# The last block's first down product among the last up products, read from PSUM by VectorE

## The chip, the cores and the metric

One core of a Trainium2 chip runs the whole program. The metric is device time in microseconds (us), from the first to the last instruction and what lies around them, as the median of several executions. Smaller is better.

## The reference

The reference is a two-layer trunk over 512 tokens of 1024 channels in fp32: a mixer, cross-attention into 256 memory tokens, and a squared-ReLU MLP in each layer, every one behind an RMSNorm, with a final RMSNorm. What matters here is the MLP, which both layers have:

```
def squared_relu_mlp(h, w1, w2):          # h (512 x 1024), w1 (1024 x 4096), w2 (4096 x 1024)
    return jnp.square(jax.nn.relu(h @ w1)) @ w2
...
h = rmsnorm(x, norm_ffn_g[i])
x = x + squared_relu_mlp(h, ffn_w1[i], ffn_w2[i])
...
return rmsnorm(x, final_norm_g)
```

## The kernel before

**Blocks and products.** The 4096 hidden channels are worked in FB = 4 blocks of 1024, numbered 0 to 3. A block has an up product (`"U"`, tokens x 1024 by 1024 x 1024) and a down product (`"D"`). Each is a 2 x 2 block matrix product done with seven quarter-size products, P1 to P7, instead of eight (Winograd's form): the operands of some are sums of quarters, the results of several are accumulated in one pair of PSUM banks and read at stages. Each product has two halves and each half is one *step*: 12 matmuls of 128x512 for a down step, 24 matmuls of 128x256 for an up step. fp32 accuracy comes from three matmuls on operands split in a high and a low part: ScalarE writes the high part of a weight (`w_hi`, L748), VectorE the low part (`w_lo`, L1253), and the same for activations (`slot_hi` L762, `slot_lo` L1263).

**Weights.** The split weights lie in a ring of RING = 4. `ahead(kind, b, p, half)` makes the split for the step three behind the named one (AHEAD = 3), so ScalarE writes a split when TensorE has finished the step four before it. The raw quarter of a weight comes from HBM into a buffer: `sum` (`w_sum[:, 0:2]`), `22` and `21`. In the `sum` buffer P1 uses the quarter 11 as loaded; then GpSimd issues an accumulating DMA (`add_quarters`, L1942) that adds the next quarter in place, for P5, then for P6, then P4. In `22`, P3 uses what was loaded and P7 what it is after one addition. An addition may start when the split of the step before it has been made (`wlo_ready`). SP loads the next block's quarters when the last reader of a buffer has made its split (`refill`, L633).

**Order.** The order of steps is written out by hand and every engine follows it: `ORDER` for the blocks, `LAST_UPS` for the stretch where up products of block 3 alternate with down products of block 2, `LAST_DOWN` for the rest of block 3. There P1 of block 3 comes second, behind half of P2: 466.44 us is the first matmul of D P4 of block 2 in layer 0, and P2.0, P1.0, P1.1, P5.0, P5.1, P3.0, P3.1, P6.0, P6.1, P2.1, P7.0, P7.1, P4.0, P4.1 follow it.

**Results.** Down results are added to the residual rows in `y_rows` in SBUF. For most, VectorE reads PSUM, scales and adds (`read`, L1621). Three of a layer are *staged* (`STAGED`): ScalarE scales PSUM into `staged` in SBUF (`stage`, L979), and GpSimd issues a DMA that adds it to `y_rows` (`add_staged`, L1953). They are P4 of block 2 and P1 and P5 of block 3. P3 of block 3 goes on accumulating in the PSUM banks of P5, so TensorE waits before P3.0, tile by tile, until P5 has been staged; P6 accumulates behind P1, P7 behind P6, P4 behind P7, each after the reading before it.

**Queues.** ScalarE, VectorE, GpSimd and SP each work strictly in their written order. In ScalarE's, the splits for P3.1 and P6.0 stand around the staging of P1 and before that of P5. In GpSimd's, the additions for P5, P3 and P6 of block 3 have a staged one behind P1's, P5's and P3's.

**Start of the MLP.** Up P5 of block 0 is kept in SBUF in two halves by ScalarE (`keep`, L925, counting `kept_half` and `kept_ready`). TensorE waits before step U P3.0 for the first half, and for `sum_done(0, "P2")`, which is VectorE's sum at L1538.

**Behind the MLP of layer 0.** The rows are transposed back into tiles (`tiles_from_rows`) in banks that `mlp_order` and `walk` name, and the gate product `sv` starts in banks that must have been copied out.

Of the kernel before, what the change touches and what calls it, by code (L numbers as in the profile page):

```python
# [22 lines left out]
ALU = mybir.AluOpType  # L23
# [33 lines left out]
LAST_DOWN = (("P2", 0), ("P1", 0), ("P1", 1), ("P5", 0), ("P5", 1), ("P3", 0), ("P3", 1), ("P6", 0), ("P6", 1),  # L57
             ("P2", 1), ("P7", 0), ("P7", 1), ("P4", 0), ("P4", 1))
LAST_UPS = (("D", "P1"), ("U", "P1"), ("D", "P2"), ("U", "P2"), ("D", "P5"), ("U", "P5"), ("D", "P3"), ("U", "P3"),
            ("U", "P6"), ("D", "P6"), ("U", "P7"), ("D", "P7"), ("U", "P4"), ("D", "P4"))  # L60
READS = {b: ("P1", "P2", "P5", "P3", "P6", "P7", "P4") for b in range(FB - 2)}
READS[FB - 2] = ("P1", "P2", "P5", "P3", "P6", "P7")
READS[FB - 1] = ("P3", "P6", "P2", "P7", "P4")
STAGED = ((FB - 2, "P4"), (FB - 1, "P1"), (FB - 1, "P5"))


def mlp_steps():

    steps = [("U", 0, p, h) for p in ORDER for h in range(2)]
    for b in range(FB - 2):  # L70
        for p in ORDER:
            steps += [("D", b, p, h) for h in range(2)] + [("U", b + 1, p, h) for h in range(2)]
    steps += [(kind, FB - 2 + (kind == "U"), p, h) for kind, p in LAST_UPS for h in range(2)]
    return tuple(steps + [("D", FB - 1, p, h) for p, h in LAST_DOWN])

# [24 lines left out]
LAST_SLOTS = {"P2": 0, "P5": 1, "P1": 2, "P3": 2, "P6": 1, "P7": 2, "P4": 1}  # L100
# [51 lines left out]
class Numbers:  # L152
# [64 lines left out]
    def walk(self):  # L217
# [84 lines left out]
    def mlp_order(self, l):  # L302
# [37 lines left out]
def trunk_kernel(nc, x_t, x_rows, mem_t, weights, up_d, down_d, gains_d, ws_t, bs_d, lng_d, lnb_d, ident_d, band_d, last_gain_d, out):  # L340
# [90 lines left out]
    staged = [at(a_off + 16 * KB + 4 * KB * i, f"staged_{i}", [P, 2, 512]) for i in range(3)]  # L431
# [90 lines left out]
    quarter_added = [sem(f"quarter_added{i}") for i in range(4)]  # L522
    up_loaded = [sem(f"up_loaded{i}") for i in range(6)]
# [14 lines left out]
    rows_added = sem("rows_added")  # L538
# [41 lines left out]
    def buffer(kind, i):  # L580

        if kind == "D":
# [39 lines left out]
    with nc.Block() as block:  # L622

        @block.sync
        def _(sp):
# [3 lines left out]
            def quarter(l, kind, b, name, half):  # L629
# [3 lines left out]
                sp.dma_start(buffer(kind, i), source[FB * l + b, 2 * QUARTERS.index(name) + half]).then_inc(loaded[i], 16)  # L633
# [46 lines left out]
            def mlp_loads(l):  # L680
# [44 lines left out]
        def _(act):  # L725
# [10 lines left out]
            def hi_quarter(c):  # L736
# [6 lines left out]
                if added == 0:  # L743
                    act.wait_ge(loaded[i], 16 * (FB * l + b + 1))
                else:
                    sums = 3 if part == "sum" else 1
                    act.wait_ge(adds[i], 16 * (sums * (FB * l + b) + added))
                act.activation(w_hi[:, c % RING, :], buffer(kind, i), ACT.Copy).then_inc(whi_ready, 1)  # L748
# [165 lines left out]
            def mlp(l):  # L914
# [180 lines left out]
                stage(1)  # L1095
                ahead("D", b, "P5", 1)
                stage(2)
# [132 lines left out]
        def _(dve):  # L1230
# [15 lines left out]
            def lo_any(c):  # L1246
# [6 lines left out]
                dve.tensor_tensor(w_lo[:, c % RING, :], buffer(kind, SUM_BUFFER[STAGE[p][0]] + half),  # L1253
# [257 lines left out]
            def mlp(l, stat, norm):  # L1511
# [86 lines left out]
                def read(b, p, tile_waits=False):  # L1598
# [3 lines left out]
                    if (b, p) == (FB - 1, "P2"):  # L1602
                        dve.wait_ge(rows_added, added_count(l, 1))
                    elif (b, p) == (FB - 1, "P7"):
                        dve.wait_ge(rows_added, added_count(l, 2))
                    elif (b, p) == (FB - 1, "P4"):
                        dve.wait_ge(rows_added, added_count(l, 0))
# [139 lines left out]
                operand(c, "P1", a11)  # L1747
# [41 lines left out]
            def last_rows():  # L1789
# [775 lines left out]
```

## Time and profile before

| what | value |
|---|---|
| median of 3 runs | 1162.18 us (1161.82 to 1162.69) |
| the profiled execution, its time | 1160.81 us |
| the profiled execution, span from first to last instruction | 1159.0 us |
| TensorE busy | 1134.8 us, 98% |
| VectorE, ScalarE, GpSimd busy | 810.3, 653.6, 212.0 us |
| mean granted TensorE clock | 0.998 of full |

Busy shares are averages. TensorE's has matmuls that overlap their neighbours, so the start of a matmul less the start of the one before it says more than its duration: in an undisturbed down step these starts lie about 0.227 us apart. A row of the timeline has in brackets the idle time before an instruction and the engine and line that ended it.

### The profile page before, as it was taken

Reading aid. Unit: us, or ns where it says so; the run is one execution under the profiler, and the core shown is the slowest. Engines: PE = TensorE matmul, PEld = TensorE weight load, DVE = VectorE, ACT = ScalarE, POOL = GpSimd, SP = SyncE. Lnnn points to the kernel's source line nnn. Section 1 sums busy time; section 2 is a strip of 40 time slices with the busy share of each in tenths; the row PEclk is TensorE's granted clock in tenths of the full one; section 3 lists DMA queues with packets and bytes.
Section 4 is the critical chain, followed back from the end, with each engine's and each line's share of the span. In section 5 each row is a group of like instructions: output and inputs, shape, how many; then the busy total and the mean of one; then the engine's idle time right before and its main releaser. Section 6 shows DMA issues by size and latency. Waiting matters only on the chain.

```text
span 1159.0 us, 16201 instructions
## 1 busy us (share of the span) xinstructions
PE 1134.8 (98%) x6556; PEld 1000.2 (86%) x6556; DVE 810.3 (70%) x923; ACT 653.6 (56%) x811; POOL 212.0 (18%) x196
## 2 busy tenths in 40 slices
PE   9999999999999999899999999999999999999996
PEld 7988889999999999688888888888999999999974
DVE  7887646686786776677487645664668678677677
ACT  6764445765655565655444443544576565556565
POOL 0040012112111120212164012001311211112030
PEclk9999999999999999999999999999999999999999
DMA  9532143899789785856232622313489978978585
GB/s 353 206 97 91 50 146 73 198 245 197 190 175 213 171 153 115 214 118 198 89 98 81 217 96 73 109 37 146 77 221 231 206 182 179 211 167 153 125 157 146
DMA packets 50378, 179.75 MB, mean 155 GB/s; under 512 B 5632, under 2 KB 6016, under 8 KB 49664
## 3 DMA queue, kind: packets, MB, share of 16 engines
q0 software_dynamic: 20064, 70.26, 33.6%
q1 hardware_dynamic: 28656, 104.35, 27.1%
q10 hardware_dynamic: 1584, 4.10, 1.1%
q8 instruction: 52, 0.85, 0.3%
q14 instruction: 22, 0.18, 0.1%
HBM read 173.45 MB, written 2.10 MB: 151 GB/s over the span
## 4 chain that ended last, share of the span: by engine, by line
PE 83%; DVE 7%; ACT 4%; DMA 3%; issue 2%; POOL 1%; SPq 0%; ACTq 0%; DVEq 0%; POOLq 0%
PE psum L2004 12%; PE psum L2006 11%; PE psum L2005 11%; PE psum L2264 8%; PE psum L2266 8%; PE psum L2265 8%; PE psum L2284 7%; PE psum L2285 7%; PE psum L2286 7%; DMA w_sum<-in_down 3%; ACT w_hi L748 1%; DMA w_raw<-in_weights 1%; PE psum L2201 1%; DVE w_lo L1253 1%; PE psum L2323 1%
## 5 line engine op out<-in xcount | busy, mean ns | idle before, releaser
L1253 DVE TENSOR_TENSOR w_lo<-w_sum,w_hi 128x1024 fp32r<-128x1024 f32 x112 | 136.0, 1223 | 82.2 <-ACT w_hi L748 82.1
L2284 PE MATMUL psum<-w_lo,slot_hi 128*128 128x512 f32 x448 | 176.0, 393 | 9.8 <-ACT staged L979 5.0
L2285 PE MATMUL psum<-w_hi,slot_hi 128*128 128x512 f32 x448 | 175.5, 392 | 0.0
L2286 PE MATMUL psum<-w_hi,slot_lo 128*128 128x512 f32 x448 | 174.9, 390 | 0.0
L748 ACT ACTIVATE w_hi<-w_sum 128x1024 fp32r<-128x1024 f32 x112 | 117.6, 1054 | 93.7 <-PE psum L2286 52.8
L2264 PE MATMUL psum<-xs_s_lo,w_hi 128*128 128x256 f32 x512 | 145.4, 284 | 2.7 <-ACT kept_p L925 2.7
L2266 PE MATMUL psum<-xs_s_hi,w_lo 128*128 128x256 f32 x512 | 144.9, 283 | 0.0
L2265 PE MATMUL psum<-xs_s_hi,w_hi 128*128 128x256 f32 x512 | 144.9, 283 | 0.0
L1253 DVE TENSOR_TENSOR w_lo<-w_raw,w_hi 128x1024 fp32r<-128x1024 f32 x80 | 97.6, 1222 | 41.9 <-ACT w_hi L748 41.7
L748 ACT ACTIVATE w_hi<-w_raw 128x1024 fp32r<-128x1024 f32 x80 | 83.8, 1055 | 69.0 <-PE psum L2266 56.8
L1942 POOL DMA_DIRECT2D w_sum<-in_down x64 | 58.6, 942 | 343.9 <-DVE w_lo L1253 343.8
L2284 PEld LDWEIGHTS psum<-w_lo,slot_hi 128*128 128x128 f32 x448 | 84.7, 189 | 28.5 <-issue 10.7
L2266 PE MATMUL psum<-xs_a_hi,w_lo 128*128 128x256 f32 x384 | 108.7, 283 | 0.0
L2265 PE MATMUL psum<-xs_a_hi,w_hi 128*128 128x256 f32 x384 | 108.7, 283 | 0.0
L2264 PE MATMUL psum<-xs_a_lo,w_hi 128*128 128x256 f32 x384 | 108.6, 283 | 0.0
L2264 PEld LDWEIGHTS psum<-xs_s_lo,w_hi 128*128 128x128 f32 x512 | 98.2, 192 | 3.9 <-issue 3.0
L2286 PEld LDWEIGHTS psum<-w_hi,slot_lo 128*128 128x128 f32 x448 | 84.5, 189 | 18.0
L2265 PEld LDWEIGHTS psum<-xs_s_hi,w_hi 128*128 128x128 f32 x512 | 98.2, 192 | 0.9
L2285 PEld LDWEIGHTS psum<-w_hi,slot_hi 128*128 128x128 f32 x448 | 84.6, 189 | 15.9
L2266 PEld LDWEIGHTS psum<-xs_s_hi,w_lo 128*128 128x128 f32 x512 | 98.2, 192 | 0.0
L1239 DVE TENSOR_TENSOR w_lo<-w_raw,w_hi 128x1024 fp32r<-128x1024 f32 x58 | 76.1, 1319 | 19.5 <-ACT w_hi L734 19.5
L2004 PE MATMUL psum<-a_lo,w_hi 128*128 128x512 f32 x192 | 75.9, 395 | 0.0
(236 smaller groups left out, 2662.4 us busy)
## 6 DMA issues: line engine op xcount, KB each, us to landing
w_raw<-in_weights SPq DMA_DIRECT2D x89, 512.0 KB, 3.7
w_sum<-in_down POOLq DMA_DIRECT2D x64, 512.0 KB, 7.7
w_sum<-in_down SPq DMA_DIRECT2D x48, 512.0 KB, 4.5
w_raw<-in_up POOLq DMA_DIRECT2D x48, 512.0 KB, 6.6
w_raw<-in_up SPq DMA_DIRECT2D x32, 512.0 KB, 3.9
up<-in_up SPq DMA_DIRECT2D x16, 512.0 KB, 4.5
up<-in_up POOLq DMA_DIRECT2D x16, 512.0 KB, 6.9
y_rows<-staged POOLq DMA_DIRECT2D x6, 512.0 KB, 8.0
```

Source lines behind the costliest of these rows:

```text
L748: act.activation(w_hi[:, c % RING, :], buffer(kind, i), ACT.Copy).then_inc(whi_ready, 1)
L1239: dve.tensor_tensor(w_lo[:, slot, :], w_raw[:, raw, :], w_hi[:, slot, :].bitcast(F32), ALU.subtract).then_inc(wlo_ready, 1)
L1253: dve.tensor_tensor(w_lo[:, c % RING, :], buffer(kind, SUM_BUFFER[STAGE[p][0]] + half), w_hi[:, c % RING, :].bitcast(F32), ALU.subtract).t ...
L2004: pe.matmul(out_ap, s_hi, m_lo, start=start, stop=False)
L2005: pe.matmul(out_ap, s_hi, m_hi, start=False, stop=False)
L2006: return pe.matmul(out_ap, s_lo, m_hi, start=False, stop=stop)
L2264: pe.matmul(to, h[:, k, tile], x_lo[:, k, :], start=fresh and m == k == 0, stop=False, skip_group_check=True)
L2265: pe.matmul(to, h[:, k, tile], x_hi[:, k, :], start=False, stop=False, skip_group_check=True)
L2266: last = pe.matmul(to, lw[:, k, tile], x_hi[:, k, :], start=False, stop=(k == 3), skip_group_check=True)
L2284: pe.matmul(to, s_hi[:, k, tok], w_lo[:, c % RING, cols], start=first, stop=False, skip_group_check=True)
L2285: pe.matmul(to, s_hi[:, k, tok], w_hi[:, c % RING, cols], start=False, stop=False, skip_group_check=True)
L2286: last = pe.matmul(to, s_lo[:, k, tok], w_hi[:, c % RING, cols], start=False, stop=(kp == 1 and j == 1), skip_group_check=True)
```

## The change

P1 of block 3 is moved from the last down steps to the last up products, between D P7 of block 2 and U P4 of block 3. Its weights (and those of P5, P6, P4 of block 3 after it) no longer lie in `w_sum[:, 0:2]` but in `up_22`, the up products' buffer, free after U P7 of block 3, with semaphores `last_added` of their own. P4 of block 2 and P1 of block 3 are no longer staged; VectorE reads them. Only P5 of block 3 is staged. PSUM pairs, slots and transpose banks are renamed to fit. In the MLP's start, ScalarE keeps the first half of up P5 two instructions earlier.

```diff
-LAST_DOWN = (("P2", 0), ("P1", 0), ("P1", 1), ("P5", 0), ("P5", 1), ("P3", 0), ("P3", 1), ("P6", 0), ("P6", 1),
+LAST_DOWN = (("P2", 0), ("P5", 0), ("P5", 1), ("P3", 0), ("P3", 1), ("P6", 0), ("P6", 1),
              ("P2", 1), ("P7", 0), ("P7", 1), ("P4", 0), ("P4", 1))
+LAST_UPS = tuple((kind, FB - 2 + (kind == "U"), p) for p in ("P1", "P2", "P5", "P3") for kind in "DU") + (
+    ("U", FB - 1, "P6"), ("D", FB - 2, "P6"), ("U", FB - 1, "P7"), ("D", FB - 2, "P7"), ("D", FB - 1, "P1"),
+    ("U", FB - 1, "P4"), ("D", FB - 2, "P4"))
-STAGED = ((FB - 2, "P4"), (FB - 1, "P1"), (FB - 1, "P5"))
+STAGED = ((FB - 1, "P5"),)
-LAST_SLOTS = {"P2": 0, "P5": 1, "P1": 2, "P3": 2, "P6": 1, "P7": 2, "P4": 1}
+LAST_SLOTS = {"P1": 0, "P2": 1, "P5": 0, "P3": 2, "P6": 0, "P7": 2, "P4": 0}
-    return {PAIR_X: PAIR_A, PAIR_Y: PAIR_E if p == "P2" else PAIR_Y}[ROWS_PAIR[p]]
+    return {PAIR_X: PAIR_E, PAIR_Y: PAIR_A if p == "P2" else PAIR_Y}[ROWS_PAIR[p]]
-            self.add(("xt", m), "bank", at=(4, 5, 2, 3)[m])
+            self.add(("xt", m), "bank", at=4 + m)
-            self.row_chunk("sv", i, ST, at=(0, 1, 6, 7, 5, 2, 3, 4))
+            self.row_chunk("sv", i, ST, at=(0, 1, 2, 3, 5, 6, 7, 4))
-                self.add(("xt", m), "bank", at=(6, 7, 0, 1)[m - 4])
+                self.add(("xt", m), "bank", at=m - 4)
...
+        if (kind, b) == ("D", FB - 1) and i < 2:
+            return up_22[:, i, :]
...
@@ SP: the loads of the last block @@
+                refill(l, "D", FB - 2, "P2")
+                for half in range(2):
+                    sp.wait_ge(wlo_ready, step(l, "U", FB - 1, "P7", half) + 1)
+                    quarter(l, "D", FB - 1, "11", half)
+                refill(l, "D", FB - 2, "P7")
@@ ScalarE: start of the MLP @@
                 ahead("U", 0, "P5", 0)
+                keep(0, "P5", kept_p5, PAIR_X, half=0)
                 hi(xs["P4"][0][:], xg[:, 4:8, TOK[1]])
                 ahead("U", 0, "P5", 1)
-                keep(0, "P5", kept_p5, PAIR_X, half=0)
@@ ScalarE: the last block @@
                 ahead("U", c, "P7", 0)
-                operand(c, "P2", a12, h=1)
+                operand(c, "P1", a11, h=0)
                 ahead("U", c, "P7", 1)
-                squared(c, 2, a22, "P7")
                 ahead("D", b, "P7", 0)
                 ahead("D", b, "P7", 1)
+                squared(c, 2, a22, "P7")
+                ahead("D", c, "P1", 0)
+                operand(c, "P2", a12, h=1)
+                ahead("D", c, "P1", 1)
...
                 operand(c, "P5", s1, summed=1)
-                operand(c, "P1", a11, h=0)
                 b = FB - 1
                 ahead("D", b, "P2", 0)
-                stage(0)
-                ahead("D", b, "P1", 0)
-                ahead("D", b, "P1", 1)
                 operand(b, "P3", a12, summed=3)
                 ahead("D", b, "P5", 0)
...
-                stage(1)
                 ahead("D", b, "P5", 1)
-                stage(2)
+                stage(0)
                 operand(b, "P6", last_s2, summed=2)
@@ VectorE: the last block @@
                 read(b, "P6")
+                operand(c, "P1", a11)
+                ahead("U", c, "P7", 1)
+                ahead("D", b, "P7", 0)
+                c22(c)
+                ahead("D", b, "P7", 1)
+                ahead("D", c, "P1", 0)
+                read(b, "P7")
                 operand(c, "P2", a12)
-                ahead("U", c, "P7", 1)
-                c22(c)
-                ahead("D", b, "P7", 0)
-                ahead("D", b, "P7", 1)
+                ahead("D", c, "P1", 1)
                 ahead("U", c, "P4", 0)
-                read(b, "P7")
+                read(c, "P1")
...
                 operand(c, "P5", s1)
-                operand(c, "P1", a11)
                 b = FB - 1
                 ahead("D", b, "P2", 0)
                 last_sum_s4(b)
-                ahead("D", b, "P1", 0)
-                ahead("D", b, "P1", 1)
+                read(b - 1, "P4")
                 operand(b, "P3", a12)
+                ahead("D", b, "P5", 0)
                 sum_s3(b)
-                ahead("D", b, "P5", 0)
@@ GpSimd @@
-                        elif p != "P6":
-                            add_staged(l, ("P1", "P5", "P3").index(p))
+                        elif p == "P3":
+                            add_staged(l, 0)
@@ TensorE @@
                 down_product(b, "P7")
+                kept_done(c, "P3")
+                down_product(c, "P1", fresh=True)
                 sum_done(c, "P7")
                 up_product(c, "P4")
                 read_done(b, "P7")
                 down_product(b, "P4")
                 b = FB - 1
-                kept_done(b, "P3")
+                kept_done(b, "P4")
                 down(b, "P2", 0, fresh=True).then_inc(psum_ready, 1)
-                kept_done(b, "P4")
-                down_product(b, "P1", fresh=True)
...
-                pe.wait_ge(staged_ready, 6 * l + 4)
+                read_done(b, "P1")
                 down_product(b, "P6")
```

## Rows read from the trace of the kernel before

**Rows 1.** The page: busy us, share of the span and instructions by engine.
```profile
PE 1134.8 (98%) x6556; PEld 1000.2 (86%) x6556; DVE 810.3 (70%) x923; ACT 653.6 (56%) x811; POOL 212.0 (18%) x196
```
**Rows 2.** Waits of TensorE: who released it, us in total, times, longest.
```profile
PE psum L2284 <- ACT staged L979: 5.0, 2, 4.0
PE psum L2284 <- DVE y_rows L1621: 2.8, 2, 1.7
PE psum L2264 <- ACT kept_p L925: 2.7, 2, 1.3
PE psum L2284 <- DVE slot_lo L1263: 2.1, 2, 1.1
```
**Rows 3.** Timeline, TensorE, layer 0's last block: start, duration, instruction [idle <- releaser].
```profile
466.44 0.40 PE L2284 MATMUL psum<-w_lo,slot_hi 128*128 128x512 f32 x1
...
471.90 0.39 PE L2284 MATMUL psum<-w_lo,slot_hi 128*128 128x512 f32 x1
...
475.75 0.47 PE L2284 MATMUL psum<-w_lo,slot_hi 128*128 128x512 f32 x1 [0.96 <-DVE slot_lo L1263]
...
490.83 0.58 PE L2284 MATMUL psum<-w_lo,slot_hi 128*128 128x512 f32 x1 [3.95 <-ACT staged L979]
...
511.56 0.39 PE L2284 MATMUL psum<-w_lo,slot_hi 128*128 128x512 f32 x1
```
**Rows 4.** Windows: stretch, us, busy by engine, granted TensorE clock, DMA share, GB/s.
```profile
491.00:495.00 4.00, 4.00 (x11) 3.11 (x11) 2.73 (x3) 2.16 (x3) 2.24 (x3) 0.57 1.10 183
```
**Rows 5.** Timeline, ScalarE, the same stretch.
```profile
489.06 1.06 ACT L748 ACTIVATE w_hi<-w_sum 128x1024 fp32r<-128x1024 f32 x1 [3.81 <-DMA w_sum<-in_down]
490.02 1.25 ACT L979 ACTIVATE staged<-psum,negative_r 128x512 f32<-128x512 f32 x2
```
**Rows 6.** The chain of waits through that stretch: start, us, what.
```profile
469.88 7.74 DMA w_sum<-in_down
...
481.24 7.74 DMA w_sum<-in_down
```
**Rows 7.** Timeline, TensorE, layer 1's last block.
```profile
1101.72 0.40 PE L2284 MATMUL psum<-w_lo,slot_hi 128*128 128x512 f32 x1
...
1145.71 0.47 PE L2284 MATMUL psum<-w_lo,slot_hi 128*128 128x512 f32 x1 [1.69 <-DVE y_rows L1621]
```
**Rows 8.** Timeline, VectorE, layer 0: split for U P7.0, low part of P5's operand.
```profile
442.41 1.23 DVE L1253 TENSOR_TENSOR w_lo<-up,w_hi 128x1024 fp32r<-128x1024 f32 x1 [1.66 <-ACT w_hi L748]
...
473.25 1.22 DVE L1263 TENSOR_TENSOR slot_lo<-s,slot_hi 128x1024 fp32r<-128x1024 f32 x1
```
**Rows 9.** Timeline, ScalarE, layer 0: split for U P4.0 of block 3.
```profile
452.54 1.06 ACT L748 ACTIVATE w_hi<-w_raw 128x1024 fp32r<-128x1024 f32 x1 [0.60 <-PE psum L2266]
```
**Rows 10.** Tile staged: its DMAs, from issue to landing.
```profile
DMA to landing us min/median/max: 5.4/8.0/12.0
```
**Rows 11.** Timeline, ScalarE, layer 1: splits for P6.0 and P4.1 of block 3.
```profile
1121.55 1.06 ACT L748 ACTIVATE w_hi<-w_sum 128x1024 fp32r<-128x1024 f32 x1 [1.43 <-DMA w_sum<-in_down]
...
1141.44 1.06 ACT L748 ACTIVATE w_hi<-w_sum 128x1024 fp32r<-128x1024 f32 x1 [1.40 <-DMA w_sum<-in_down]
```
**Rows 12.** Timeline, VectorE, layer 1, before P4: gain of the first rows, reading of P7.
```profile
1143.68 1.22 DVE L1508 TENSOR_TENSOR out_rows<-y_rows,last_gain 128x1024 f32<-128x1024 f32 x1
1144.82 1.40 DVE L1621 SCALAR_TENSOR_TENSOR y_rows<-psum,negative_r,y_rows 128x512 f32<-128x512 f32 x2
```
**Rows 13.** Timeline, TensorE, first matmul of the gate product.
```profile
519.13 0.47 PE L2004 MATMUL psum<-w_lo,a_hi 128*128 128x512 f32 x1 [0.20 <-issue]
```
**Rows 14.** Timeline, TensorE, layer 0: step U P3.0 of block 0.
```profile
208.80 0.36 PE L2264 MATMUL psum<-xs_s_lo,w_hi 128*128 128x256 f32 x1 [1.33 <-ACT kept_p L925]
```
**Rows 15.** Timeline, ScalarE, before that step.
```profile
206.06 1.05 ACT L762 ACTIVATE xs_a_hi<-xg 128x1024 fp32r<-128x1024 f32 x1
...
207.96 0.58 ACT L925 ACTIVATE kept_p<-psum 128x512 f32<-128x512 f32 x1
```
**Rows 16.** Timeline, VectorE, before that step: the sum of up P1 and P2.
```profile
206.58 1.22 DVE L1538 TENSOR_TENSOR a<-psum,kept 128x1024 f32<-128x1024 f32 x1
```

More of the change, by code:

```diff
@@ L72, in mlp_steps @@
             steps += [("D", b, p, h) for h in range(2)] + [("U", b + 1, p, h) for h in range(2)]
-    steps += [(kind, FB - 2 + (kind == "U"), p, h) for kind, p in LAST_UPS for h in range(2)]
+    steps += [(kind, b, p, h) for kind, b, p in LAST_UPS for h in range(2)]
     return tuple(steps + [("D", FB - 1, p, h) for p, h in LAST_DOWN])
@@ L430, in trunk_kernel @@
     last_s2 = at(z_off, "last_s2", [P, 4, NMEM])
-    staged = [at(a_off + 16 * KB + 4 * KB * i, f"staged_{i}", [P, 2, 512]) for i in range(3)]
+    staged = [at(a_off + 16 * KB + 4 * KB * i, f"staged_{i}", [P, 2, 512]) for i in range(len(STAGED))]
     edge_lo = at(region(GROUPS * PAD * 4), "edge_lo", [P, GROUPS, PAD], F32R)
@@ L522, in trunk_kernel @@
     quarter_added = [sem(f"quarter_added{i}") for i in range(4)]
+    last_added = [sem(f"last_added{i}") for i in range(2)]
     up_loaded = [sem(f"up_loaded{i}") for i in range(6)]
@@ L537, in trunk_kernel @@
     staged_ready = sem("staged_ready")
-    rows_added = sem("rows_added")
+    rows_added = [sem(f"rows_added{i}") for i in range(len(STAGED))]
     tile_ready = sem("tile_ready")
@@ L578, in first_raw, with buffer @@
         return N.raw[C[f"o{l}"] + 7] + 1
-    def buffer(kind, i):
+    def buffer(kind, b, i):
+        if (kind, b) == ("D", FB - 1) and i < 2:
+            return up_22[:, i, :]
         if kind == "D":
@@ L632, in quarter @@
                 source, loaded = (up_d, up_loaded) if kind == "U" else (down_d, quarter_loaded)
-                sp.dma_start(buffer(kind, i), source[FB * l + b, 2 * QUARTERS.index(name) + half]).then_inc(loaded[i], 16)
+                sp.dma_start(buffer(kind, b, i), source[FB * l + b, 2 * QUARTERS.index(name) + half]).then_inc(loaded[i], 16)
             def refill(l, kind, b, p):
@@ L744, in hi_quarter @@
                     act.wait_ge(loaded[i], 16 * (FB * l + b + 1))
-                else:
-                    sums = 3 if part == "sum" else 1
-                    act.wait_ge(adds[i], 16 * (sums * (FB * l + b) + added))
-                act.activation(w_hi[:, c % RING, :], buffer(kind, i), ACT.Copy).then_inc(whi_ready, 1)
+                elif part != "sum":
+                    act.wait_ge(adds[i], 16 * (FB * l + b + added))
+                elif kind == "U":
+                    act.wait_ge(up_added[i], 16 * (3 * (FB * l + b) + added))
+                elif b < FB - 1:
+                    act.wait_ge(quarter_added[i], 16 * (3 * ((FB - 1) * l + b) + added))
+                else:
+                    act.wait_ge(last_added[i], 16 * (3 * l + added))
+                act.activation(w_hi[:, c % RING, :], buffer(kind, b, i), ACT.Copy).then_inc(whi_ready, 1)
             def hi_any(c):
@@ L1252, in lo_any @@
                 dve.wait_ge(whi_ready, c + 1)
-                dve.tensor_tensor(w_lo[:, c % RING, :], buffer(kind, SUM_BUFFER[STAGE[p][0]] + half),
+                dve.tensor_tensor(w_lo[:, c % RING, :], buffer(kind, b, SUM_BUFFER[STAGE[p][0]] + half),
                                   w_hi[:, c % RING, :].bitcast(F32), ALU.subtract).then_inc(wlo_ready, 1)
@@ L1938, in add_quarters @@
                 source, added = (up_d, up_added) if kind == "U" else (down_d, quarter_added)
+                if kind == "D" and b == FB - 1 and part == "sum":
+                    added = last_added
                 for half in range(2):
@@ L1941, in add_quarters @@
                     pool.wait_ge(wlo_ready, step(l, kind, b, p, half) + 1)
-                    pool.dma_start(buffer(kind, i), source[FB * l + b, 2 * QUARTERS.index(name) + half],
+                    pool.dma_start(buffer(kind, b, i), source[FB * l + b, 2 * QUARTERS.index(name) + half],
                                    accum_op=ALU.add).then_inc(added[i], 16)
@@ L1948, in add_staged @@
                 part = ROWS_PART[p]
-                pool.wait_ge(rows_read, read_count(l, FB - 2, {"P4": "P7", "P1": "P2", "P5": "P7"}[p]))
-                if p == "P4":
-                    pool.wait_ge(rows_read, read_count(l, FB - 3, "P4"))
-                pool.wait_ge(staged_ready, 2 * (3 * l + i) + 2)
-                pool.dma_start(y_part(*part), staged[i][:], accum_op=ALU.add).then_inc(rows_added, 16)
+                pool.wait_ge(rows_read, read_count(l, FB - 2, "P7"))
+                pool.wait_ge(staged_ready, 2 * l + 2)
+                pool.dma_start(y_part(*part), staged[i][:], accum_op=ALU.add).then_inc(rows_added[i], 16)
             def mlp(l):
@@ L2429, in mlp @@
                     read_done(b, "P7")
-                    pe.wait_ge(staged_ready, 2)
                     tiles_from_rows(4)
```

32 lines of the change are left out of this document (10 added, 22 removed).

## The prediction

> **What bounds the kernel now.** I read the page first: TensorE is busy 98% of the span and no other engine over 70% [rows 1]. So the time is TensorE's own work, which the change leaves alone (the same steps in another order), and the places where it waits; its idle time comes to 1159.0 less 1134.8, 24 us, its end included. I then asked for TensorE's waits [rows 2]: the reader sees 12.6 us in four groups of two waits; for `y_rows` both are in layer 1, for the others there is one per layer. Three groups lie in the last block, the fourth (`kept_p`) at the start of the MLP, and the change touches all of them.
>
> Third, TensorE's timeline in layer 0 [rows 3]. From the start of D P4 of block 2 (466.44) the next two steps take 5.46 us (to 471.90), so a down step is worth 2.72 us undisturbed. Up to the last product, P4 of block 3 (511.56), lie 14 such steps, 38.1 us, but 45.1 us pass: 7.0 us are lost. They are 1.1 us before P1.0 (475.75), 4.1 us before P3.0 (490.83), and some 1.7 us behind it, because there the granted clock read 0.57 of full for 4 us [rows 4], that is mostly at the lower of its two levels, 1.2 GHz. What the engine did before the clock fell is the idle 3.95 us. In layer 1 the same 14 steps take 44.0 us [rows 7], so 5.9 us are lost there in four shorter waits of 1.0 to 1.7 us [rows 2], with no fall visible.
>
> Fourth, what ended the long wait. ScalarE staged P5 at 490.02, directly behind its split of P6.0's weights at 489.06, for which it had stood 3.81 us behind a DMA [rows 5]. The chain shows that DMA: the addition for P6.0, issued at 481.24 and 7.74 us in flight, and before it the addition for P5.0, issued at 469.88, also 7.74 us [rows 6]. So P1 split, add, P5 split, add, P6 split is one serial chain, and its start is tied to P1, whose buffer is busy until D P4 of block 2. TensorE doesn't need P6.0's weights yet: it waits for a staging that is queued behind them.
>
> **The change part by part.**
>
> *P1 two steps earlier.* TensorE's D P4 of block 2 starts 5.44 us later (466.44 becomes 471.9), P2.0 at 477.3, P5.0 at 480.05, P3.0 at 485.5. P1.0's split now takes the ring slot that U P4.0 had, at 452.5 [rows 9]; its addition is issued some 3 us later, near 456, and is wanted for P5.0's split near 472. With 7.74 us in flight [rows 6] it is there 8 us early. P5.0's split takes P1.0's old place in the pattern, 5.44 us later, so its addition is issued at 469.88 + 5.44 = 475.3. It lands at 483.0 with 7.74 us, at 480.7 with the 5.4 us that is the shortest landing of a like DMA [rows 10]. P6.0's split can't start before 484.2 for another reason (below). The 4.1 us wait loses its cause.
>
> *P1's load.* SP may issue it when U P7.0 is split, at 442.41 + 1.23 = 443.6 [rows 8]; the split wants it at 452.5 [rows 9]. It has 8.9 us. The rows show no load of this kind late there; if it took the 12.0 us of the longest landing in rows 10, the stall would be 3.1 us.
>
> *P5's operand.* Its low part ended at 473.25 + 1.22 = 474.47 [rows 8], behind U P4 and the square. It moves with U P4 by 5.44 us to 479.9, and TensorE wants it at 480.05. So the 1.1 us wait, which was for P1's low part queued one operation behind, goes to about nothing; bounds 0 and 0.3 us.
>
> *What is late next.* P3.0 waits for the staging of P5. ScalarE's order before it: P3's operand, split P3.1, split P6.0, staging. P3's operand waits for VectorE, which after 479.9 makes the split of P3.0 and the sum for P3, 1.14 us apart in a busy VectorE: done 482.2. Then three ScalarE operations at 0.96 us each (489.06 to 490.02 in [rows 5]): staging of the first tile starts at 485.15, ends 485.8, and TensorE follows 0.15 us later, at 485.95 where it wanted 485.5. I take 0.45 us as the new wait, per layer; bounds 0 and 1.5 us (a late addition).
>
> *VectorE's new readings.* It reads P1 and P4 of block 2, 1.40 us each [rows 12], where ScalarE staged both. The one of P1 falls at about 468.5, between two splits that wait for ScalarE anyway. The one of P4 stands between the sum for P3 and P3's low part: that ends at 484.6, before 485.5. If its cover were gone it would cost 1.4 us. Nothing else of TensorE's waits for either: P6 waits for P1's reading 20 us later.
>
> *Two staged DMAs fewer.* From the landing that released P6.0's split in layer 1 (1121.5) to the one that released P4.1's (1141.4) seven GpSimd DMAs landed, 2.84 us each [rows 11]; the queue was full, so every split there stood behind it. After, the additions and the one staging are issued at (layer 0's scale) 475.3, 478.5, 482.0, 486.7, 487.4, 488.9 and 491.2. With 5.6 us for one alone and 2.84 us between two in a full queue, the last two land at 497.7 and 500.6. Their splits are wanted at 496.8 and 499.6, but TensorE starts P4 only at 505.0. In layer 0 this costs nothing. In layer 1 VectorE does 1.22 us of gain before it reads P7 [rows 12]; the split of P4.1 ends near 503.3, the gain at 504.4, and the first tile of P7 is read at 505.2, against a wanted 504.9. I take 0.5 us; bounds 0 and 3.
>
> At this place the Trainium skill speaks against the change ("DMA: Bandwidth & Descriptors", Issuing engines are not separate DMA queues): transfers from the SP, ScalarE and GpSimd queues run on the same 16 engines and interleave. By it ScalarE's load of the last gain in layer 1, issued just ahead of the additions, pushes them back by up to one service time, and the 0.5 us would be some 3; the row of the window above has the engines' share at 1.1 with GpSimd's DMAs in flight, which agrees that there is no room beside a full queue.
>
> *Sum in the last blocks.* Layer 0: 7.0 less 0.45 is 6.6 us. The clock's 1.7 us is in it: with no wait over 1.7 us left, the layer 1 block shows no fall. Layer 1: 5.9 less 0.45 less 0.5, and less 0.3 because VectorE's tail behind the reading of P7 sits 0.3 us later against TensorE's than now: 4.65 us.
>
> *Keeping half of up P5 earlier.* ScalarE kept it at 207.96, behind two operations from 206.06 on [rows 15]; now it does so at 206.06 and is done at 206.65. TensorE started at 208.80 [rows 14] and wanted 207.3. But it also waits for VectorE's sum, 206.58 to 207.80 [rows 16], so it starts at 207.95: 0.85 us gained, 1.7 us in two layers. Bounds 0 and 3.0 (1.5 each). ScalarE's operations behind it keep their times, as it never idled there.
>
> *Gate product.* It idled 0.20 us before its first matmul [rows 13], behind the copy of the tile in its bank, which is now the first copied instead of the third: 0.35 us with the start-up of the matmul; bounds 0 and 0.4.
>
> Sum: 6.6 + 4.65 + 1.7 + 0.35 = 13.3 us. Against the profiled execution's own time (1160.81, span 1159.0) that is 1147.5; this execution lies 1.4 us below the median, so on the median 1162.18 the forecast is 1148.9 us.
>
> **The rivals.**
>
> *A: the wait comes back at the same place.* P6.0's split still stands before the staging in ScalarE's order. If P5.0's addition lands 12.0 us after issue [rows 10] instead of 5.4 to 7.7, that is 487.3, the staging ends at 489.1, TensorE waits 3.7 us and the clock falls as before: 5.4 us back in layer 0 less the 0.45 counted, as much in layer 1. For it: many landings were that long. Against: those were behind a full queue, and at 475.3 this one is alone. Gain left 13.3 - 10 = 3.3 in both layers, 8.3 in one: 1153.9 to 1158.9 us.
>
> *B: the last additions are late.* They are issued from 489 to 491 behind P3's and the staged one. With landings of 12 us the split of P4.1 ends at 505.5 and the reading of P7 slips 1.5 us in layer 0 and 2.7 in layer 1: 4 us less the 0.5 counted, so 1152.4 us. For it: rows 11, and the skill's rule above. Against: two staged DMAs fewer are ahead of them, and P5's additions are out of the queue by then.
>
> *C: slower than before.* P1's load sits in front of everything: split, addition, and ScalarE's whole queue wait for it. It has 8.9 us, and each us more is a us of TensorE in each layer. It cancels the gain when it lands 8.9 + 6.7 = 15.6 us after issue in both; at 18 us the kernel would take 1148.9 + 2 x 9.1 = 1167 us. The longest landing of the rows is 12.0 us.
>
> *D: no change.* TensorE at 98% is its own bound and what is taken from one wait appears in the next engine's order, because ScalarE and VectorE have no room for operations in another order. VectorE's 70% [rows 1] speaks against it. 1162 us.
>
> **How the numbers follow.** Forecast (gain 11 to 16 us, all bounds of the small terms) 0.63; A 0.12; B 0.15; C 0.05; D 0.05. If every bound falls well, the gain is 7.0 + 5.9 + 3.0 + 0.4 = 16.3 us, 1145.9; the range reaches on the other side through B and one layer of A: 1145.8 to 1155.0. What a measurement of this kernel can tell from no change is about 0.2%, 2.3 us. Faster: forecast, A, B and a little of D, 0.91. Same 0.04, slower 0.05.
>
> **What would show it.** In the changed kernel's profile TensorE's wait behind `staged` should be under 1 us in each layer, the window with a clock of 0.57 gone, the waits behind `kept_p` gone and one of some 0.6 us behind L1538 in their place, ScalarE's waits for `w_sum` DMAs in the last block (the 3.81 us one first) gone or shifted to the last two splits. From D P4 of block 2 to P4 of block 3 there should be 33 us in layer 0. I would be wrong if TensorE waits at D P1 of block 3 (its load), at U P4 behind VectorE, or if a wait over 3 us is left anywhere in the last block.

## The result, and the profile after

| | before | after |
|---|---|---|
| median of the runs side by side, us | 1162.43 (1161.82 to 1165.84, 4 runs) | 1147.90 (1147.83 to 1148.66, 4 runs) |
| profiled execution, us | 1160.81 | 1147.92 |
| its span, us | 1159.0 | 1146.0 |
| its mean granted clock | 0.998 | 0.999 |

The changed kernel takes 0.9871 of the time before (95% interval 0.9851 to 0.9890): 14.5 us less by the medians, 12.9 us less between the two profiled executions. The forecast was 1148.9 us, in a range from 1145.8 to 1155.0.

The page of the changed kernel, its engines and its GpSimd queue, answers to [rows 1]. TensorE has as many matmuls as before and is busy 2.3 us less; the queue carries 68.17 MB, against 70.26 in the kernel before.

```profile
PE 1132.5 (99%) x6556; PEld 998.9 (87%) x6556; DVE 815.6 (71%) x931; ACT 648.9 (57%) x803; POOL 207.0 (18%) x192
...
q0 software_dynamic: 18976, 68.17, 33.0%
```

TensorE's waits in it (released by, us in total, times, longest) answer to [rows 2]:

```profile
PE psum L2084 <- DVE warm L1369: 1.5, 1, 1.5
PE psum L2203 <- DVE probs L1482: 1.3, 2, 0.6
PE psum L2006 <- DVE w_lo L1248: 1.1, 2, 0.7
PE psum L2266 <- issue: 0.9, 2, 0.4
PE psum L2006 <- DVE mem_lo L1269: 0.4, 1, 0.4
```

All four groups of [rows 2] are gone, 12.6 us of named waits. The one at L2266 is what is left before U P3.0 of block 0. The last line, at the start of the program, stood nowhere in the list of before.

TensorE's timeline in the last block of layer 0, against [rows 3]: start, duration, instruction.

```profile
471.49 0.40 PE L2286 MATMUL psum<-w_lo,slot_hi 128*128 128x512 f32 x1
...
484.99 0.39 PE L2288 MATMUL psum<-w_hi,slot_lo 128*128 128x512 f32 x1
485.50 0.47 PE L2286 MATMUL psum<-w_lo,slot_hi 128*128 128x512 f32 x1
...
504.64 0.39 PE L2286 MATMUL psum<-w_lo,slot_hi 128*128 128x512 f32 x1
...
511.62 0.39 PE L2288 MATMUL psum<-w_hi,slot_lo 128*128 128x512 f32 x1
511.85 0.39 PE L2006 MATMUL psum<-w_lo,a_hi 128*128 128x512 f32 x1
```

The rows are D P4 of block 2 (471.49), D P3.0 of block 3 (485.50), D P4 of block 3 (504.64) and the gate product (511.85). From the first to the third 33.15 us pass, where 33 were forecast and twelve undisturbed steps of 2.72 us [rows 3] take 32.6. Matmuls follow each other every 0.23 us, so the start at 485.50 instead of 485.22 is 0.28 us lost: too short for the trace to print as a wait, but there. The gate product follows its predecessor without a gap, unlike in [rows 13].

The windows of it (us, busy by engine, clock, DMA share, GB/s). The first spans the place of the old 4 us wait, the second is that of [rows 4], which had the clock at 0.57:

```profile
484.00:488.00 4.00, 3.88 (x18) 2.91 (x17) 4.00 (x5) 3.94 (x5) 1.92 (x3) 1.00 0.70 110
491.00:495.00 4.00, 4.00 (x19) 3.30 (x19) 3.73 (x5) 3.04 (x3) 0.08 (x1) 1.00 1.10 194
```

The clock is granted in full, and 19 matmuls start where 11 did. ScalarE in layer 0 answers to [rows 5, 9]:

```profile
452.15 1.06 ACT L756 ACTIVATE w_hi<-up 128x1024 fp32r<-128x1024 f32 x1 [0.60 <-PE psum L2268]
...
481.83 1.06 ACT L770 ACTIVATE slot_hi<-a 128x1024 fp32r<-128x1024 f32 x1 [3.61 <-DVE a L1582]
482.79 1.04 ACT L756 ACTIVATE w_hi<-w_sum 128x1024 fp32r<-128x1024 f32 x1
483.74 1.04 ACT L756 ACTIVATE w_hi<-up 128x1024 fp32r<-128x1024 f32 x1
484.69 1.42 ACT L987 ACTIVATE staged<-psum,negative_r 128x512 f32<-128x512 f32 x2
```

The split of P1.0 stands where that of U P4.0 stood. The split of P6.0 (483.74) no longer waits for a DMA; ScalarE's long idle time is now 3.61 us behind VectorE's sum for P3, and the four operations behind it run without a pause. That is the new chain before P3.0: VectorE's sum, P3's operand, two splits, the staging.

In layer 1, TensorE before P3.0 and before P4, against [rows 7]:

```profile
1112.36 0.39 PE L2288 MATMUL psum<-w_hi,slot_lo 128*128 128x512 f32 x1
1112.90 0.47 PE L2286 MATMUL psum<-w_lo,slot_hi 128*128 128x512 f32 x1
...
1131.83 0.39 PE L2288 MATMUL psum<-w_hi,slot_lo 128*128 128x512 f32 x1
1132.24 0.47 PE L2286 MATMUL psum<-w_lo,slot_hi 128*128 128x512 f32 x1
```

Lost: 0.31 us and 0.18 us, against 5.9 us in the whole block before. One split there still waits for an addition, that of P4.1 on ScalarE (against [rows 11]):

```profile
1127.46 1.06 ACT L756 ACTIVATE w_hi<-up 128x1024 fp32r<-128x1024 f32 x1 [1.30 <-DMA up<-in_down]
```

and it sets VectorE's readings of P7 before P4 (against [rows 12]):

```profile
1129.08 1.22 DVE L1259 TENSOR_TENSOR w_lo<-up,w_hi 128x1024 fp32r<-128x1024 f32 x1
1130.21 1.22 DVE L1514 TENSOR_TENSOR out_rows<-y_rows,last_gain 128x1024 f32<-128x1024 f32 x1
1131.35 0.74 DVE L1623 SCALAR_TENSOR_TENSOR y_rows<-psum,negative_r,y_rows 128x512 f32<-128x512 f32 x1
```

Last, U P3.0 of block 0 in both layers, on TensorE (against [rows 14]):

```profile
208.43 0.36 PE L2266 MATMUL psum<-xs_s_lo,w_hi 128*128 128x256 f32 x1 [0.43 <-issue]
...
835.84 0.35 PE L2266 MATMUL psum<-xs_s_lo,w_hi 128*128 128x256 f32 x1 [0.43 <-issue]
```

### The profile page after: what moved, and what is told of

The parts are those of the page before. It is cut to its first block, busy times and chain, and to the rows that moved or that the text cites. A ratio compares the mean times of both kernels' runs of the same rounds, so it can differ in the third digit from the quotient of the medians.

```text
span 1146.0 us, 16195 instructions
## 1 busy us (share of the span) xinstructions
PE 1132.5 (99%) x6556; PEld 998.9 (87%) x6556; DVE 815.6 (71%) x931; ACT 648.9 (57%) x803; POOL 207.0 (18%) x192
## 3 DMA queue, kind: packets, MB, share of 16 engines
q0 software_dynamic: 18976, 68.17, 33.0%
## 4 chain that ended last, share of the span: by engine, by line
PE 90%; DVE 6%; ACT 2%; issue 1%; DMA 1%; POOL 0%; SPq 0%; DVEq 0%; POOLq 0%; ACTq 0%
PE psum L2006 12%; PE psum L2007 12%; PE psum L2008 12%; PE psum L2266 9%; PE psum L2268 9%; PE psum L2267 9%; PE psum L2286 8%; PE psum L2287 8%; PE psum L2288 8%; DMA w_raw<-in_weights 1%; PE psum L2203 1%; DVE w_lo L1259 1%; PE psum L2325 1%; DVE w_lo L1248 1%; POOL sq L1995 0%
## 5 line engine op out<-in xcount | busy, mean ns | idle before, releaser
L1259 DVE TENSOR_TENSOR w_lo<-w_sum,w_hi 128x1024 fp32r<-128x1024 f32 x96 | 116.9, 1223 | 65.2 <-ACT w_hi L756 65.1
L2266 PE MATMUL psum<-xs_s_lo,w_hi 128*128 128x256 f32 x512 | 145.4, 284 | 0.9 <-issue 0.9
L756 ACT ACTIVATE w_hi<-w_sum 128x1024 fp32r<-128x1024 f32 x96 | 101.2, 1055 | 69.6 <-PE psum L2288 56.4
L2266 PE MATMUL psum<-xs_a_lo,w_hi 128*128 128x256 f32 x384 | 108.6, 283 | 0.0
L2266 PEld LDWEIGHTS psum<-xs_s_lo,w_hi 128*128 128x128 f32 x512 | 98.1, 192 | 2.1 <-issue 1.2
L1946 POOL DMA_DIRECT2D w_sum<-in_down x52 | 44.8, 862 | 290.6 <-DVE w_lo L1259 290.4
```

Of the source, the lines that this page charges most:

```text
L756: act.activation(w_hi[:, c % RING, :], buffer(kind, b, i), ACT.Copy).then_inc(whi_ready, 1)
L1259: dve.tensor_tensor(w_lo[:, c % RING, :], buffer(kind, b, SUM_BUFFER[STAGE[p][0]] + half), w_hi[:, c % RING, :].bitcast(F32), ALU.subtract ...
L2266: pe.matmul(to, h[:, k, tile], x_lo[:, k, :], start=fresh and m == k == 0, stop=False, skip_group_check=True)
```

## The experiments

The theory under test: before, one serial chain on ScalarE and the GpSimd queue (P1 split, add, P5 split, add, P6 split, staging) started too late, and the change starts it two steps earlier; the missing staged DMAs matter less (unstaged_only and moved_staged show how far that holds). Seven kernels, each beside runs of the kernel before.

| kernel | median, us | of before | ratio (95%) |
|---|---|---|---|
| keep_only | 1160.61 | 1161.93 | 0.9989 (0.9980 to 0.9997) |
| before_swap | 1161.36 | 1161.93 | 0.9995 (0.9985 to 1.0005) |
| unstaged_only | 1153.40 | 1161.93 | 0.9921 (0.9908 to 0.9935) |
| moved_staged | 1148.50 | 1162.77 | 0.9879 (0.9865 to 0.9894) |
| late_load | 1147.69 | 1162.77 | 0.9874 (0.9859 to 0.9889) |
| after_swap | 1146.96 | 1161.93 | 0.9870 (0.9856 to 0.9883) |
| swap_gain_early | 1146.85 | 1162.77 | 0.9867 (0.9851 to 0.9884) |

### keep_only: the earlier keeping alone

```
+                keep(0, "P5", kept_p5, PAIR_X, half=0)
                 hi(xs["P4"][0][:], xg[:, 4:8, TOK[1]])
                 ahead("U", 0, "P5", 1)
-                keep(0, "P5", kept_p5, PAIR_X, half=0)
```

> The kernel before with one edit: ScalarE keeps the first half of up P5 two instructions earlier. My step says TensorE's wait at step U P3.0 of block 0 shrinks to what VectorE's sum leaves, 0.85 us less in each layer: 1.7 us less in all, near 1160.6 us if before is 1162.3. Rival: TensorE waits for something else there to the same moment, 0 us. Upper bound, both waits gone: 3.0 us.

Measured: 1.3 us less, with an interval of 0.3 to 2.3, in which the 1.7 expected lies. TensorE at U P3.0, and in its last blocks:

```profile
207.97 0.36 PE L2264 MATMUL psum<-xs_s_lo,w_hi 128*128 128x256 f32 x1 [0.43 <-issue]
...
490.25 0.60 PE L2284 MATMUL psum<-w_lo,slot_hi 128*128 128x512 f32 x1 [4.16 <-ACT staged L979]
...
1144.35 0.47 PE L2284 MATMUL psum<-w_lo,slot_hi 128*128 128x512 f32 x1 [1.98 <-DVE y_rows L1621]
```

U P3.0 starts 0.83 us earlier than in [rows 14], and its wait is 0.9 us shorter in both layers; the waits in the last blocks are all still there. The term holds by itself. In layer 1 the wait before P4 is 1.98 us instead of the 1.69 of [rows 7], and the clock falls behind it (window of this kernel). That takes the gain back in this one profiled execution, whose span is 1159.2 us:

```profile
1145.50:1149.50 4.00, 4.00 (x13) 3.11 (x12) 2.82 (x6) 2.52 (x8) 0.00 (x0) 0.57 0.00 2
```

### before_swap: is it the order on ScalarE alone?

The long wait was a staging queued behind a split that TensorE didn't need yet. So the cheapest cure would be to exchange the two.

```
                 stage(1)
-                ahead("D", b, "P5", 1)
                 stage(2)
+                ahead("D", b, "P5", 1)
```

> The kernel before with P5's staging ahead of the split of P6.0 in ScalarE's order, nothing else. Rival theory, the order of ScalarE's queue alone made the loss: the 4.1 us wait before P3.0 and the clock's 1.7 us go in layer 0, some 5.4 us less in layer 0 and 0.7 in layer 1, near 1156 us. My theory, a full queue of accumulating DMAs stands behind it: the wait before P3.0 goes, but P6's additions still land at about 505 and 507, VectorE's split of P4.1 ends near 509.8 and P7 is read only behind it, so TensorE starts P4 at about 510.7 instead of 511.56: under 1.5 us less in layer 0 and nothing in layer 1, near 1161.3 us.

Measured: no difference that can be told (ratio 0.9995, the interval holds 1). The wait before P3.0 did go, and came back later: from D P1.0 to D P4.0 of block 3 the profiled execution needs 35.37 us, where the kernel before needs 35.81. TensorE in layer 0:

```profile
494.03 0.47 PE L2284 MATMUL psum<-w_lo,slot_hi 128*128 128x512 f32 x1 [0.67 <-DVE slot_lo L1263]
504.83 0.50 PE L2284 MATMUL psum<-w_lo,slot_hi 128*128 128x512 f32 x1 [2.35 <-DVE y_rows L1621]
```

ScalarE behind it shows why, with the additions late one after the other:

```profile
498.65 1.06 ACT L748 ACTIVATE w_hi<-w_sum 128x1024 fp32r<-128x1024 f32 x1 [2.79 <-DMA w_sum<-in_down]
501.13 1.06 ACT L748 ACTIVATE w_hi<-w_sum 128x1024 fp32r<-128x1024 f32 x1 [1.42 <-DMA w_sum<-in_down]
...
506.37 1.06 ACT L748 ACTIVATE w_hi<-w_sum 128x1024 fp32r<-128x1024 f32 x1 [3.23 <-DMA w_sum<-in_down]
509.00 1.06 ACT L748 ACTIVATE w_hi<-w_sum 128x1024 fp32r<-128x1024 f32 x1 [1.58 <-DMA w_sum<-in_down]
```

In layer 1 this execution took 2.0 us longer than before between U P3.0 of block 0 and P4 of block 3, with 2.59 us of idle time before P4, but also with 1.82 us before P1.0, ahead of the exchanged operations, and a fall of the clock behind it; one trace doesn't say what of this is the edit's.

The rival (the order alone is the cause) is out. The chain through the GpSimd queue was late as a whole; the staging was only the place where TensorE felt it first.

### unstaged_only: VectorE reads two results, P1 stays where it was

```
-STAGED = ((FB - 2, "P4"), (FB - 1, "P1"), (FB - 1, "P5"))
+STAGED = ((FB - 1, "P5"),)
...
-                stage(0)
                 ahead("D", b, "P1", 0)
...
+                read(b, "P4")
                 b = FB - 1
                 ahead("D", b, "P2", 0)
...
                 ahead("D", b, "P5", 1)
+                read(b, "P1")
```

> The kernel before with P4 of block 2 and P1 of block 3 read by VectorE instead of staged (two accumulating DMAs fewer per layer); P1 stays where it was, as do its weights' buffer and the other orders. My theory: the addition for P6.0 is issued at about 480.9 and lands at 486.6 instead of 489.0, TensorE starts P3.0 at 488.5 (a wait of 1.8 us, no fall of the clock), and the last additions land 4 us earlier: 4.1 us less in layer 0, some 3.5 in layer 1, the 1.1 us wait before P1.0 stays in both, near 1154.8 us. Rival, the earlier start of P1's chain is the whole gain: the wait before P3.0 stays near 4 us and the kernel is within 2 us of before.

Measured: 8.5 us less, where 7.6 were expected (4.1 and 3.5); the two profiled spans differ by 7.5. TensorE in layer 0, then ScalarE:

```profile
475.80 0.47 PE L2275 MATMUL psum<-w_lo,slot_hi 128*128 128x512 f32 x1 [0.96 <-DVE slot_lo L1260]
488.39 0.47 PE L2275 MATMUL psum<-w_lo,slot_hi 128*128 128x512 f32 x1 [1.43 <-ACT staged L978]
```

```profile
486.62 1.06 ACT L747 ACTIVATE w_hi<-w_sum 128x1024 fp32r<-128x1024 f32 x1 [1.83 <-DMA w_sum<-in_down]
487.58 1.25 ACT L978 ACTIVATE staged<-psum,negative_r 128x512 f32<-128x512 f32 x2
```

The wait before P1.0 in layer 0 is that of [rows 3] to a hundredth (in layer 1 it is 1.39 us, before 1.10): it belongs to P1's place, not to the staging. The one before P3.0 fell from 3.95 to 1.43 us, as the addition for P6.0, issued at 480.94, was there 5.7 us later and not 7.74 [rows 6]; and behind 1.43 us the clock did not fall. So the chain is the same, and the emptier queue shortens it.

### moved_staged: P1 moved and with its own buffer, three results still staged

```
-STAGED = ((FB - 1, "P5"),)
+STAGED = ((FB - 1, "P1"), (FB - 2, "P4"), (FB - 1, "P5"))
...
-                read(c, "P1")
...
-                read(b - 1, "P4")
```

(An edit of the changed kernel; P1's result is staged as the first, its P4 as the second.)

> The changed kernel with all three results staged again (P1 of block 3 behind the split for D P4.1 of block 2, P4 of block 2 behind the split of P3.0), so P1 and its weights' buffer are moved but the two accumulating DMAs are back. Together with the run that only unstaged it says how the two parts share the gain. My theory: P1's staging falls into an empty queue and costs nothing; P4's one puts 2.8 us more in front of P3's and P6's additions, which layer 0 has in hand and layer 1 has not: layer 0 as in the changed kernel, layer 1 some 2.5 us later, near 1150.5 us. So either part alone gives most of the gain, because both empty the same queue. Rival: the parts add up, the move is worth what the unstaged kernel lacked (4 us) and no more, so 14.0 less 8.5 less 1.3 is 4.2 us below before plus the kept half's 1.3, near 1156.5 us.

Measured: 1148.5 us, 14.3 less than before and within 0.6 of the changed kernel, which the intervals don't tell apart. My own number was 2 us too pessimistic, and the additive rival's 8 us. What staging still costs is seen in layer 1, TensorE and then ScalarE:

```profile
1133.31 0.47 PE L2295 MATMUL psum<-w_lo,slot_hi 128*128 128x512 f32 x1 [0.84 <-DVE y_rows L1630]
```

```profile
1126.58 1.06 ACT L757 ACTIVATE w_hi<-up 128x1024 fp32r<-128x1024 f32 x1 [1.11 <-DMA up<-in_down]
1129.05 1.06 ACT L757 ACTIVATE w_hi<-up 128x1024 fp32r<-128x1024 f32 x1 [1.41 <-DMA up<-in_down]
```

The split of P4.0 waits for its addition too, and P4 starts 0.99 us late instead of 0.18. So the move, with its own buffer, takes out nearly everything. The two halves of the change cure the same waits: alone they are worth 8.5 us and (with the keeping and the gate) 14.3 us, together 14.5. That the missing staged DMAs matter less holds only once the chain starts early.

No run gives P1 a buffer of its own in its old place, so the move and the buffer are tested as one. ScalarE's rows of the kernel before, P1.0's split in layer 0 and in layer 1, say that the buffer alone would do little:

```profile
466.64 1.06 ACT L748 ACTIVATE w_hi<-w_sum 128x1024 fp32r<-128x1024 f32 x1 [1.82 <-PE psum L2266]
...
1102.06 1.06 ACT L748 ACTIVATE w_hi<-w_sum 128x1024 fp32r<-128x1024 f32 x1 [1.96 <-DMA w_sum<-in_down]
```

In layer 0 the split waited last for TensorE, that is for its place in the ring, which goes by the order of steps; only in layer 1 did the load into `w_sum` come last.

### late_load: SP loads P1 one place later

```
                 refill(l, "D", FB - 2, "P2")
+                refill(l, "D", FB - 2, "P7")
                 for half in range(2):
-                    sp.wait_ge(wlo_ready, step(l, "U", FB - 1, "P7", half) + 1)
                     quarter(l, "D", FB - 1, "11", half)
-                refill(l, "D", FB - 2, "P7")
```

(In the changed kernel, the load of P1 goes behind the refill for D P7 of block 2.)

> The changed kernel with SP loading P1's weights of block 3 behind both loads of the 22 quarter, so they are issued at about 452.1 us instead of 443.3 and land at about 457 to 458.5, where ScalarE wants to split them at 452.15. The prediction's pricing of a late load (each us past its slack of 8.9 us is a us of TensorE in each layer): some 5 us more per layer, near 1158 us. My theory now: the price forgot the ring; a split is wanted 8 us before TensorE uses it, the low part ends at 459.3 and TensorE starts D P1 at 460.3, and what is queued behind it on ScalarE and VectorE has 3 us or more in hand: 0 to 0.5 us, near 1148.2.

Measured: 1147.69 us, 0.2 less than the changed kernel, where the prediction's rival C priced such a delay at some 10. The load is issued 8.9 us later than in the changed kernel (443.27 there). SP, then ScalarE:

```profile
452.14 0.91 SPq L632 DMA_DIRECT2D up<-in_down  x2
```

```profile
457.51 1.06 ACT L755 ACTIVATE w_hi<-up 128x1024 fp32r<-128x1024 f32 x1 [6.08 <-DMA up<-in_down]
458.74 1.07 ACT L755 ACTIVATE w_hi<-up 128x1024 fp32r<-128x1024 f32 x1 [0.17 <-DMA up<-in_down]
```

TensorE at D P1.0 of block 3:

```profile
460.17 0.39 PE L2285 MATMUL psum<-w_lo,slot_hi 128*128 128x512 f32 x1
```

The split waits 6.08 us, and TensorE loses nothing: D P1.0 is the third of the down steps that begin at 454.71, and it starts 5.46 us behind the first, as in the changed kernel (454.83 and 460.30, 5.47). The low part of its split, begun at 458.61, takes 1.23 us and is done 0.3 us before. In the changed kernel that split starts at 452.15, some 8 us before its product: three steps. So the load has the 8.9 us and about 5.4 more, the delay of the split.

### after_swap: the last chain on ScalarE shortened

```
-                ahead("D", b, "P5", 1)
                 stage(0)
+                ahead("D", b, "P5", 1)
```

(The exchange of before_swap, in the changed kernel.)

> The changed kernel with P5's staging ahead of the split of P6.0 in ScalarE's order. What is left of TensorE's wait before P3.0 is 0.3 us in each layer, behind ScalarE. VectorE makes the low part of P6.0 only at 486.4, so a split that ends at 486.0 instead of 484.7 costs nothing. Expected 0.6 us less than the changed kernel, 1147.3. Rival: P6's additions slip and layer 1 gives the 0.6 us back, 1147.9.

Measured: 1146.96 us, 0.9 less than the changed kernel's median, though the two ratios to the kernel before (0.9870 and 0.9871) don't tell them apart. TensorE runs through P3.0 at 0.23 us a matmul in both layers, so the wait left there was that order. In layer 1 it returns before P4:

```profile
1131.48 0.47 PE L2286 MATMUL psum<-w_lo,slot_hi 128*128 128x512 f32 x1 [0.58 <-DVE y_rows L1623]
```

Of the 1.0 us between the two spans (1146.0 and 1145.0), 0.54 stood before U P3.0 of layer 0 already, where the two programs are the same: the matmul ahead of its wait began at 207.72 in the changed kernel and at 207.18 here. Some 0.4 us came by the end of layer 0's last block (gate product at 511.85 and 510.94). So the exchange is worth about 0.4 us of the 0.6 expected, an estimate from one trace each; half of what the medians show is not its work.

### swap_gain_early: the gain's load moved off the additions

```
                 ahead("U", c, "P6", 1)
+                if l:
+                    act.dma_start(last_gain[:], last_gain_d.partition_broadcast(P)).then_inc(gain_loaded, 16)
                 ahead("D", b, "P6", 0)
...
-                if l:
-                    act.dma_start(last_gain[:], last_gain_d.partition_broadcast(P)).then_inc(gain_loaded, 16)
```

(On top of after_swap.)

> The changed kernel with P5's staging ahead of P6.0's split, and layer 1's load of the last gain (512 KB, ScalarE's queue) issued behind the split for D P6.0 of block 2 instead of in front of P6's additions. In the kernel with the swap alone TensorE still waits 0.6 us in layer 1 before P4, behind a split that waits for a DMA. My theory: the gain's load holds up the last additions by up to 2.8 us, without it the split of P4.1 is on time: 0.7 us less than the swap alone, 1146.3 us. Rival: the additions are paced by their own queue, and it stays at 1147.0.

Measured: 1146.85 us, 0.1 below after_swap, which is inside the noise. Before P4 in layer 1 TensorE now shows:

```profile
1130.75 0.39 PE L2288 MATMUL psum<-w_hi,slot_lo 128*128 128x512 f32 x1
1131.16 0.47 PE L2286 MATMUL psum<-w_lo,slot_hi 128*128 128x512 f32 x1
```

That is 0.18 us lost, where after_swap lost 0.7. The additions are in time sooner once the load is gone: from the issue of P4.1's to its split 8.99 us pass, in after_swap 9.86. But the span of both profiled executions is 1145.0: a longer wait at the start of the program (0.8 us behind `mem_lo` instead of 0.6) took part of it. By its median it lies 1.0 us below the changed kernel.

## Why the prediction was right

Taken from starts in the two timelines of TensorE, the terms come out as follows. The end of the last VectorE instruction moved by 13.2 us, the span by 13.0; the other 0.2 lies in the writing of the output.

| term | forecast, us | measured, us | from |
|---|---|---|---|
| last block, layer 0 | 6.6 | 6.55 | P4 at 511.56, then 504.64, less the 0.37 gained ahead of it |
| gate product | 0.35 | 0.36 | 7.57 and 7.21 from P4 to it |
| last block, layer 1, with the tail | 4.65 | 4.96 | P4 at 1145.71, then 1132.24, less 8.24 ahead of it; tail -0.27 |
| keeping, both layers | 1.7 | 1.86 | 0.90, and 0.96 from 7.28 at the gate product to 8.24 at U P3.0 of layer 1 |
| start of the program | 0 | -0.53 | U P3.0 of layer 0 moved by only 0.37 |
| sum | 13.3 | 13.2 | |

The sum fits better than its parts. Two terms came out 0.3 and 0.2 us larger than forecast, and the start, put at nothing, took 0.53 back. The start of one and the same program scatters by more than that (*Left open*), so this much of the agreement is luck.

*The chain.* Right in mechanism and size: P5.0's addition, forecast for 475.3, was issued at 474.31; ScalarE's split of P6.0 free of the DMA; the wait before P1.0 at zero. Its start was tied to P1 by more than the buffer, which the prediction named: in layer 0 it was P1's place in the ring that its split waited for last (see moved_staged). unstaged_only and moved_staged split the cause: the wait before P1.0 hangs on the move alone, the one before P3.0 on both.

*What is late next.* The 0.45 us before P3.0 were 0.28 and 0.31. The order of operations was as worked out (sum for P3, P3's operand, two splits, staging). VectorE ran ahead of the forecast, and after_swap shows that this order was all that was left there.

*The clock.* No wait over 1.7 us was forecast, and no fall; both hold. The 1.7 us that the fall behind the old wait cost in layer 0 are therefore in the gain.

*VectorE's readings.* Costed at nothing. The trace agrees: the reading of P4 began at 481.71, P3's low part behind it ended at 484.25, before the 485.22 at which TensorE would have wanted it. moved_staged can't show it by itself, as it brings the two DMAs back with the staging.

*Two staged DMAs fewer.* The term that I knew least: 0.5 us (0 to 3) before P4 in layer 1, measured 0.18, with the gain's load still in front of the additions; 0.99 with three staged. Rival B, last additions 4 us late, did not come: the split of P4.1 waited 1.30 us. The rule of the Trainium skill weighed there ("DMA: Bandwidth & Descriptors", Issuing engines are not separate DMA queues) has the right direction: without the gain's load beside them the additions let P4 start some 0.5 us earlier (swap_gain_early against after_swap). The 3 us worked out for it were six times too much even there, and in the changed kernel the whole wait was 0.18 us.

*The keeping.* Bound on its other side by VectorE's sum, as said: of 1.49 us lost in layer 0, 0.59 stay. VectorE's sum (L1544 in the changed kernel) ran from 207.11 to 208.33, and TensorE started at 208.43. The trace puts the wait down to `issue` and not to the sum, as the prediction expected; why is not shown.

*Where the prediction failed: rival C's price.* It said "each us more is a us of TensorE in each layer". late_load delayed the load by 8.9 us and cost nothing that can be seen. The split is made about three steps before TensorE needs it, and what stands behind it in ScalarE's queue has such a lead as well, so the first 5 us of lateness fall into it. With that slack a landing of 15 us would not have cancelled the gain, and the 0.05 for a slower kernel was too much.

*Why the medians moved more than the profiles.* The profiled execution of before was among its quickest. Of 21 runs of it beside keep_only, the ten with a mean clock of 0.994 or 0.995 have a median of 1162.8 us, the seven with 0.997 or 0.998 one of 1161.6. The changed kernel's runs have 0.997 to 0.999 and lie within 0.83 us of each other. That kernels with waits of 2 to 4 us lose a clock period more often than the one profile shows fits this, and keep_only and before_swap show such falls at new places; that it is the whole 1.6 us is not shown. The forecast's last step, the profile's gain taken off the median, is thus the one that missed by 1.0 us.

*Left open.* The 0.3 to 0.8 us behind `mem_lo` at the start appear in the profiles of all kernels with P1's own buffer and not in the others. But the start scatters by as much without it: the matmul ahead of the wait before U P3.0 of layer 0 began at 207.19 in the kernel before and at 208.20 in before_swap, whose program is the same up to there, and between 207.18 and 207.98 in the kernels with the buffer. So the traces don't tie it to the change, and nothing was run to find its cause.

## What to carry to other kernels

When an engine waits for an operation that is queued behind a late transfer, follow the transfer back through what had to be done to issue it. If that is a serial chain through several engines, exchanging two operations at its end only moves the wait (before_swap); start the chain earlier. And before pricing a late input one for one, count how many steps ahead of its use the first operation on it is made.

## What the runs showed of the hardware

- The granted clock fell behind TensorE's idle times of 4.16, 3.95, 2.35, 1.98 and 1.82 us, and not behind 1.69 or 1.43. It also did not fall behind one of 2.59 us (before_swap, layer 1). So the length of the wait alone doesn't decide. Windows of before_swap, behind 2.35, 1.82 and 2.59 us:

```profile
505.50:509.50 4.00, 4.00 (x13) 3.14 (x11) 2.45 (x4) 1.55 (x2) 0.00 (x0) 0.57 0.59 116
1113.50:1117.50 4.00, 4.00 (x12) 3.10 (x12) 3.29 (x3) 2.22 (x4) 2.22 (x3) 0.58 0.36 65
1149.00:1153.00 4.00, 4.00 (x19) 3.27 (x18) 3.75 (x9) 3.60 (x9) 0.00 (x0) 1.00 0.01 2
```

- An accumulating GpSimd DMA of 512 KB into a nearly empty queue was there in 5.7 us (unstaged_only). In a full one they arrive 2.5 us apart or a little more (the splits of P4.0 and P4.1 in moved_staged, both released by their DMA, start 2.47 us apart; the seven landings of [rows 11] were 2.84 us apart in the mean). What the queue costs depends on when it is filled: four staged DMAs fewer (two results in two layers, read by VectorE instead) moved the time by 0.6 us with the chain early, which is inside the intervals, and by 8.5 with the chain late.
